# A hybrid trunk's state-space scan: the skip term's diagonals on GpSimd, the carried state copied by VectorE

## What is computed

```python
def ssd_chunk_scan(x, dt, a_head, bmat, cmat, s0):       # chunks of 128 tokens
    a_cs = cumsum(dt * a_head)                           # in a chunk
    decay = exp(where(lower, a_cs[l] - a_cs[s], -inf))
    y_diag = einsum((cmat @ bmat) * decay, x * dt)
    chunk_states = einsum(bmat, exp(a_cs[-1] - a_cs), x * dt)
    s_in, s_final = scan(s * exp(a_cs[-1]) + chunk_states, s0)
    return y_diag + einsum(cmat, s_in, exp(a_cs)), s_final

y = y_f + flip(y_b) + xs * p['d'][:, None]               # 'd': the skip term
y = y.reshape(bsz, n, SSD_DI) * silu(z)
```

## Time and profile before

| | us |
|---|---|
| median of 3 runs (1158.30 to 1163.59) | 1160.81 |
| the profiled execution, its own time | 1160.04 |
| its span, first to last instruction | 1158.2 |
| the scan within it, about | 757.9 to 863.8 |

### The profile page before, as it was taken

The page is one execution under the profiler, slowest core; times in us unless marked ns, Lnnn a source line. Parts: engine busy times, 40 slices in busy tenths (PEclk is TensorE's granted clock), DMA queues, the critical chain, the costliest instruction groups (busy, mean ns, idle before and its releaser), DMA issues.

```text
span 1158.2 us, 16832 instructions
## 1 busy us (share of the span) xinstructions
PE 1065.1 (92%) x5726; PEld 835.6 (72%) x5726; DVE 674.9 (58%) x1124; ACT 644.0 (56%) x1155; POOL 312.5 (27%) x265
## 2 busy tenths in 40 slices
PE   5899998899899999999799999978878989999997
PEld 1785654446857888887499999957767976778885
DVE  1432663434355999996565640177766134798994
ACT  2523432445245887886555452398775424588880
POOL 0520920003202000001436655655556600100000
PEclk9899999999988999999899999998898999899999
DMA  9643527993139999995323333476630304999973
GB/s 385 237 182 145 200 109 284 423 420 132 64 114 358 411 411 411 411 409 199 140 73 113 110 111 143 148 214 188 189 119 1 145 1 161 378 412 410 411 311 128
DMA packets 86368, 266.71 MB, mean 230 GB/s; under 512 B 7329, under 2 KB 39585, under 8 KB 73249
## 3 DMA queue, kind: packets, MB, share of 16 engines
q1 hardware_dynamic: 78496, 243.30, 55.6%
q0 software_dynamic: 2880, 12.58, 2.9%
q10 hardware_dynamic: 4928, 10.01, 2.4%
HBM read 245.68 MB, written 15.47 MB: 225 GB/s over the span
## 4 chain that ended last, share of the span: by engine, by line
PE 71%; ACT 8%; DMA 8%; DVE 7%; POOL 3%; issue 2%; SPq 0%; ACTq 0%; POOLq 0%; DVEq 0%
PE bank L2117 16%; PE bank L2118 16%; PE bank L2119 16%; PE bank L2141 3%; PE bank L2401 3%; POOL wlo L736 2%; PE bank L2203 2%; ACT seg L1349 2%; PE bank L2659 2%; DMA h_blk<-h_rows,tok_of 2%; DMA modb<-modb 1%; PE bank L2376 1%; ACT whi L883 1%; DMA rowb<-acs_rows 1%; DMA modw<-wide_mods 1%
## 5 line engine op out<-in xcount | busy, mean ns | idle before, releaser
L736 POOL TENSOR_TENSOR wlo<-raw,whi 128x512 fp32r<-128x512 f32 x152 | 201.0, 1356 | 264.7 <-ACT whi L883 258.9
L2117 PE MATMUL bank<-hhi,whi 128*128 128x384 f32 (+1 forms) x504 | 176.9, 351 | 12.9 <-DVE hlo L1471 9.5
L2118 PE MATMUL bank<-hlo,whi 128*128 128x384 f32 (+1 forms) x504 | 173.3, 344 | 0.0
L2119 PE MATMUL bank<-hhi,wlo 128*128 128x384 f32 (+1 forms) x504 | 173.0, 343 | 0.0
L1849 DVE TENSOR_TENSOR wlo<-raw_more,whi 128x1024 fp32r<-128x1024 f32 x108 | 128.7, 1222 | 14.4 <-ACT whi L1146 12.9
L1849 DVE TENSOR_TENSOR wlo<-raw,whi 128x1024 fp32r<-128x1024 f32 x108 | 128.2, 1221 | 10.3 <-ACT whi L1146 8.1
L1146 ACT CAST whi<-raw_more 128x1024 fp32r<-128x1024 f32 x108 | 111.5, 1049 | 29.6 <-PE bank L2119 25.4
L1146 ACT CAST whi<-raw 128x1024 fp32r<-128x1024 f32 x108 | 111.5, 1053 | 22.6 <-PE bank L2119 12.3
L2117 PE MATMUL bank<-whi,blk_hi 128*128 128x512 f32 x288 | 115.1, 400 | 0.0
L2118 PE MATMUL bank<-wlo,blk_hi 128*128 128x512 f32 x288 | 113.8, 395 | 0.0
L2119 PE MATMUL bank<-whi,blk_lo 128*128 128x512 f32 x288 | 113.7, 395 | 0.0
(11 more groups left out here) (355 smaller groups left out, 1996.6 us busy)
## 6 DMA issues: line engine op xcount, KB each, us to landing
raw<-stream SPq DMA_DIRECT2D x56, 1024.0 KB, 4.8
raw<-experts SPq DMA_DIRECT2D x108, 512.0 KB, 11.4
raw_more<-experts SPq DMA_DIRECT2D x108, 512.0 KB, 11.3
modw<-wide_mods SPq DMA_DIRECT2D x37, 1024.0 KB, 12.5
rowb<-acs_rows SPq DMA_DIRECT2D x48, 256.0 KB, 5.2
shared<-shared SPq DMA_DIRECT2D x6, 1024.0 KB, 6.1
h_next<-h_blk SPq DMA_DIRECT2D x9, 512.0 KB, 10.6
y_rows<-y_sb ACTq DMA_DIRECT2D x9, 512.0 KB, 6.7
```

The costliest lines, as they stand in the source:

```text
L736: ins = pool.tensor_tensor(wlo[:, q % SPL, w], raw[:, pos % RAW, w], whi[:, q % SPL, w].bitcast(F32), ALU.subtract)
L2117: pe.matmul(dst, whi_, xhi_, start=first, stop=False)
L2118: pe.matmul(dst, whi_, xlo_, start=False, stop=False)
L2119: return pe.matmul(dst, wlo_, xhi_, start=False, stop=last)
```

## The change

The two diagonals of each head group are made by GpSimd, with a multiply by a per-partition scalar; those of head group hg + 1 stand right behind that group's `xw`, those of head group 0 ahead of GpSimd's first `xw`. The wait for the outputs of two head groups earlier, which used the same buffer, moves with them; one wait for VectorE's early dt work (`dt_by_dve`) is added in head group 0. The copy of the carried state leaves ScalarE's queue and becomes a VectorE copy right behind `next_state`, with its wait for the earlier stores.

```diff
@@ gpsimd
+            def skip_weights(hg):
+
+                if hg >= 2:
+                    finished(pool, JOB[f"y{hg - 2}_2"])
+                for c in range(2):
+                    pool.tensor_scalar(dskip[hg % 2 * 2 + c][:, :], k("ident"), v("ssd_d", 2 * hg + c, 1), None,
+                                       ALU.mult).then_inc(dskip_ready, 1)
+
             pool.wait_ge(wdt_ready, 1)
             pool.wait_ge(conv_out, 24)
+            skip_weights(0)
             finished(pool, JOB["z15"])
...
                 if hg + 1 < 2 * SSD_G:
                     weighted_x(hg + 1, 0)
                     weighted_x(hg + 1, 1)
+                    if hg == 0:
+                        pool.wait_ge(dt_by_dve, 4)
+                    skip_weights(hg + 1)
@@ scalar
-            def skip_weights(hg):
-
-                if hg >= 2:
-                    finished(act, JOB[f"y{hg - 2}_2"])
-                for c in range(2):
-                    act.activation(dskip[hg % 2 * 2 + c][:, :], k("ident"), ACT.Copy,
-                                   scale=v("ssd_d", 2 * hg + c, 1)).then_inc(dskip_ready, 1)
...
-            skip_weights(0)
             gate_out(XCH - 2)
...
-                    if t == 0:
-
-                        if hg:
-                            act.wait_ge(pf_out, 32 * hg)
-                        out_of(f"st{hg}_0", (pf[:, :], bk(JOB[f"st{hg}_0"])[:, 0:512]))
                     if t == 1 and hg + 1 < 2 * SSD_G:
                         turned_out(hg + 1)
-                        skip_weights(hg + 1)
@@ vector
                 if t == 0:
                     next_state(hg)
+                    if hg:
+                        dve.wait_ge(pf_out, 32 * hg)
+                    took(dve.tensor_copy(pf[:, :], bk(JOB[f"st{hg}_0"])[:, 0:512]), JOB[f"st{hg}_0"])
```

## The result

The changed kernel takes 1173.97 us (median of three runs, 1171.09 to 1175.31) against 1160.81 (1158.3 to 1163.59): a ratio of 1.0116, 95% interval 1.0092 to 1.0139. It is slower, as forecast, by more than forecast: 13.2 us between the medians where 8.2 stood, and the median lies 0.5 us above the range. Timed once more beside the last experiments, the same kernel took 1171.36 (six runs, 1169.56 to 1172.76) against 1160.08, a ratio of 1.0095 [1.0076, 1.0114]. The profiled execution took 1171.09, 11.05 more than the profiled one of before; its span is 1169.1 against 1158.2. What follows explains these 10.9 us of span.

A forecast was written before the change was run, and what follows sets the result against it. Loops of waits, no full engine, bound the scan; the moved copy makes VectorE, SP and broadcast a 14.0 us loop. Six of 14.0 plus one of 17.8, and the first copy, add 8.8 us: forecast 1169 us, range 1160.5 to 1173.5.

The forecast's parts named there:

- The mechanism: In the scan, VectorE's copy, SP's queue, the broadcast landing and VectorE's clamp close one loop, 14.0 us against 13.4 before.
- near 19: VectorE's idle time before its clamps, ended by broadcasts, should rise from 6.5 us to near 19.
- start of the scan: Before the scan's first exponential at 757.89 us; forecast 0, as the first two diagonals ahead of it give nothing.
- from there to the first copy's end: Head group 0, scan start to the end of VectorE's first state copy: 0.7 us more, for the copy itself.
- a loop without the weight piece, mean of six: From one VectorE state copy to the next through SP, broadcast and clamp, with no 1 MB weight load between: 14.0 us.
- the loop with the weight piece: The one copy-to-copy loop in which SP also issues a 1 MB weight load before the broadcasts: 17.8 us.
- seven loops, against 93.8: Scan from head group 0 to 7: six loops of 14.0 and one of 17.8, 102 us in all.
- tail: After the last state copy, TensorE finishes the last head group's tiles 1 and 2; forecast no change.
- From there to the last gating at 863.38 and on nothing changes: From the last copy to the last gating and all that follows, durations stay as in the old trace: 0 us.
- the rival by GpSimd: Diagonals on GpSimd come late for TensorE, 1.2 us in seven head groups: 8 us above the forecast, 1177 us; chance 4%.
- Price nothing: TensorE's transposes in every other head group wait for the copy's bank, but later outputs wait for a mask anyway: 0.
- The upper end: Top of the range: slower broadcast landings add 3.0 us, another weight piece 1.7, giving 13.5 us more; 1173.5 taken.

## Where the prediction was wrong, and what of it held

**The mechanism held.** Four of the five signs that it named are there: the copies stand 13.8 to 15.7 us apart, VectorE waits 18.8 us before its clamps ("near 19"), ScalarE's row exponentials 25.8 for the clamps (6.1 before), and SP's first store follows VectorE's copy at once (the last but one copy ends at 853.23, the store goes out at 853.26). Putting the copy back, putting the stores later and adding a slot each took the loss away, or all but 2.5 us of it. The fifth is not there: the chain goes copy, SP, broadcast, clamp in two of seven loops, not in nearly every one. And the 18.8 is near 19 in part by luck: 3.3 of it are waits for the broadcast for tile 2, which the prediction did not have.

**Term by term**, against the profiled execution:

| term of the sum | forecast, us | measured, us |
|---|---|---|
| start of the scan | 0 | +1.1 |
| from there to the first copy's end | +0.7 | +1.1 |
| a loop without the weight piece, mean of six | 14.0 | 14.24 |
| the loop with the weight piece | 17.8 | 15.65 |
| seven loops, against 93.8 | +8.1 | +7.3 |
| tail | 0 | +1.7 |
| rest of the span | 0 | -0.2 |
| sum, as put and as measured | +8.8 | +10.9 |

*The step that failed* is "From there to the last gating at 863.38 and on nothing changes", a term put at nothing that measured 1.7 us. The last head group's outputs wait for the masks that VectorE makes behind its copy; TensorE stood for 3.64 us instead of 2.84, and the same 76 matmuls then took 6.04 us busy instead of 4.37, at a clock of 0.78 instead of 1.00. The change timed again has the same 7.76 us and 0.78. The tail was copied from a trace in which TensorE was less idle ahead of it. The prediction had the earlier trace rows with a clock of 0.89 in front of it and let no term depend on the clock. The start of the scan, 1.1 us, is a second such term; why it came later stays open.

*The loops came out near by two errors that cancel.* The second broadcast behind the copy landed after 5.0 to 6.5 us, 5.2 in the first two loops, so the 5.3 was well taken. But the prediction does not have the third loop, which made the loop of head group 2 longer by 1.8 us and was as long as the forecast's in the four behind it. The third loop goes through the slot that a broadcast needs, not through SP's order alone. In head group 2 its length is 1.2 for the masks, 4.1 for the outputs, 0.4 for SP, 6.2 for the landing, 2.8 for clamp and state update and 0.6 for the copy, 15.3; with outputs of 2.2 it would be 13.4, an estimate. The prediction asked only which broadcast stands behind the copy in SP's queue, and not which ones wait for outputs that the copy delays. Against that, the weight piece held its loop for 15.65 us, not 17.8, which is 2.2 less: the broadcast behind it landed after 6.45 us where the kernel before had 8.66, and it was the next broadcast, for tile 2, that took 7.98.

*The small prices.* The copy took 0.684 us, as taken. A pair of diagonals took 1.2 us, the upper bound, not 0.6; it cost nothing, since the diagonals alone are not slower than before (2.6 us less), so the rival by GpSimd fell. The first pair took 3.07 us, ahead of the scan. "Price nothing" for TensorE's transposes was close: they waited 4.7 us in three odd head groups, ahead of outputs that wait for the mask behind the same copy by 0.4 more.

*The medians.* From the profiled execution to the median the prediction allowed 0.8 us, as in the kernel before; here it is 2.9, since the three runs of the changed kernel lie 0 to 4.2 above the profiled one. So the profiled execution came out 2.3 above its forecast of 1168.8, which is the tail and the start of the scan less what the loops gave back, and the median 4.4 above its 1169.6, where the other 2.1 is within what runs of this kernel differ by: six more have their median at 1171.36, inside the range. The upper end was worked out on both bases, 1173.5 and 1174.3, and the lower one taken; the measured 1173.97 lies between them.

## What to carry to other kernels

Before an operation is moved into another engine's queue, list every transfer that may be issued only after it, the ones that wait for its buffer and also the ones that wait for the consumers it delays, and follow each back to the engine that now holds it; where one returns to that engine, the move has closed a loop, and its length is a landing plus that engine's work. A free queue is worth less than a free slot here: the same move lost 11 to 13 us with four row slots and won 5.5 with five. When a wait ahead of a stretch of TensorE grows, its old duration may be no price for it any more.

## What the runs showed of the hardware

- GpSimd takes as long to scale a 128x128 tile by a value per partition (0.604 us) as to multiply 128x256 elements of two tensors (0.612); half the columns were no cheaper. Its first pair in the program took 3.07 us.
- VectorE copies 512 columns out of PSUM in 0.684 us, ScalarE in 0.58: the copy became dearer by the move.
- The last 76 matmuls of the scan span 7.76 us at a granted clock of 0.78, in two traces of the change, and 6.09 at 1.00 in the kernel before; with ten repeats at the head of the stretch 6.10 at 1.00. Ahead of them TensorE had waited 3.64 us in the first two, 2.84 in the third and 0.78 in the last. A wait of 3.02 us at the same place, in the change with the stores later, was followed by full clock and 6.10 us, so these waits are too near one another to tell from the last one alone which clock follows.
